# Two layers of mixers on one core: the recurrence's output projection as three one-pass products over split operands

## The reference

```
out = (yn + bonus) * g                 # 512 x 1024, from the recurrence
y   = out @ w_out                      # w_out: 1024 x 1024
x   = layernorm(ALPHA * x + (1 + gt1) * y, ln_g, ln_b)
hin = x * (1 + sc2) + sh2              # input of the feed-forward block ff0
y   = (silu(hin @ w_gate) * (hin @ w_up)) @ w_down
```

## Time and profile before

| | |
|---|---|
| time, median of three runs | 2893.52 us |
| lowest and highest run | 2893.15 and 2893.71 us |
| span of the profiled execution (first to last instruction) | 2893.6 us |
| TensorE busy | 2759.3 us, 95% |
| weight loads of TensorE | 2007.4 us, 69% |
| VectorE busy | 1360.4 us, 47% |
| ScalarE busy | 1013.0 us, 35% |
| GpSimd busy | 300.0 us, 10% |
| mean granted clock of TensorE | 0.976 |

### The profile page before, as it was taken

How to read it: one execution, slowest core, us unless ns; L and a number is a source line. 1 busy time by engine, 2 the same in 40 slices (tenths; PEclk the granted TensorE clock), 3 DMA queues, 4 the chain that set the end, 5 groups by cost and what they waited for, 6 DMA issues and landing times.

```text
span 2893.6 us, 46447 instructions
## 1 busy us (share of the span) xinstructions
PE 2759.3 (95%) x19096; PEld 2007.4 (69%) x19096; DVE 1360.4 (47%) x2285; ACT 1013.0 (35%) x1570; POOL 300.0 (10%) x250
## 2 busy tenths in 40 slices
PE   7999998899999989989999999999999899999999
PEld 3566666468888634678888778888465567788886
DVE  6566566253333257663333444433244776344335
ACT  5334333144332223644432332222011574232223
POOL 3232323010000002310000010000000131000000
PEclk9999999999999999999999999999999999999999
DMA  5334333222232111022232122232021002222331
GB/s 223 108 125 137 131 124 119 102 88 101 90 117 86 61 52 51 10 94 96 92 112 100 64 73 101 91 111 106 32 102 58 1 9 78 90 101 87 114 111 59
DMA packets 46292, 261.07 MB, mean 90 GB/s; under 512 B 5128, under 2 KB 7576, under 8 KB 26168
## 3 DMA queue, kind: packets, MB, share of 16 engines
q1 hardware_dynamic: 45128, 254.23, 25.0%
q10 hardware_dynamic: 1008, 4.57, 0.4%
HBM read 256.63 MB, written 2.15 MB: 89 GB/s over the span
## 4 chain that ended last, share of the span: by engine, by line
PE 89%; DVE 4%; ACT 3%; POOL 1%; issue 1%; DMA 1%; SPq 0%; DVEq 0%; ACTq 0%; POOLq 0%; PEld 0%; PEldq 0%
PE psum L214 87%; PE psum L2064 2%; DMA ada_first<-in_ada_first 1%; POOL branch_in L564 1%; POOL ysum L562 0%; DVE residual L1539 0%; ACT L608 0%; POOL join L557 0%; DVE residual L1531 0%; ACT yg L642 0%; DVE Y_pairs L770 0%; ACT ln_in L1494 0%; ACT nsa_probs L2100 0%; DVE ln_stat L1523 0%; DMA weights<-in_cmp_w 0%
## 5 line engine op out<-in xcount | busy, mean ns | idle before, releaser
L1657 ACT ACTIVATE ffn_weights_hi<-weights 128x1024 fp32r<-128x1024 f32 (+1 forms) x128 | 145.9, 1142 | 490.7 <-PE psum L214 490.7
L214 PE MATMUL psum<-ffn_in_hi,ffn_weights_hi 128*128 128x512 f32 x768 | 304.8, 397 | 12.4 <-DVE ffn_weights_lo L1660 7.8
L214 PE MATMUL psum<-ffn_in_hi,ffn_weights_lo 128*128 128x512 f32 x768 | 301.8, 393 | 0.0
L214 PE MATMUL psum<-ffn_in_lo,ffn_weights_hi 128*128 128x512 f32 x768 | 301.8, 393 | 0.0
L1657 ACT ACTIVATE ff_weights_hi<-weights 128x1024 fp32r<-128x1024 f32 (+1 forms) x120 | 137.7, 1147 | 433.4 <-PE psum L214 433.4
L214 PE MATMUL psum<-ff_in_hi,ff_weights_hi 128*128 128x512 f32 x704 | 277.4, 394 | 11.5 <-DVE ff_in_lo L1545 7.2
L214 PE MATMUL psum<-ff_in_lo,ff_weights_hi 128*128 128x512 f32 x704 | 276.5, 393 | 0.0
L214 PE MATMUL psum<-ff_in_hi,ff_weights_lo 128*128 128x512 f32 x704 | 276.2, 392 | 0.0
L1660 DVE TENSOR_TENSOR ff_weights_lo<-weights,ff_weights_hi 128x1024 fp32r<-128x1024 f32 (+1 forms) x116 | 156.2, 1347 | 253.5 <-ACT ff_weights_hi L1657 253.5
L1660 DVE TENSOR_TENSOR ffn_weights_lo<-weights,ffn_weights_hi 128x1024 fp32r<-128x1024 f32 (+1 forms) x126 | 166.9, 1326 | 110.5 <-ACT ffn_weights_hi L1657 110.5
L214 PEld LDWEIGHTS psum<-ffn_in_hi,ffn_weights_hi 128*128 128x128 f32 x768 | 146.2, 190 | 47.5 <-DVE ffn_weights_lo L1660 9.1
(11 more groups left out here) (519 smaller groups left out, 4878.4 us busy)
## 6 DMA issues: line engine op xcount, KB each, us to landing
weights<-in_ff_in SPq DMA_DIRECT2D x44, 1024.0 KB, 4.7
weights<-in_ffn_in SPq DMA_DIRECT2D x44, 1024.0 KB, 4.7
weights<-in_ada SPq DMA_DIRECT2D x80, 512.0 KB, 3.5
weights<-in_ff_out SPq DMA_DIRECT2D x16, 1408.0 KB, 6.0
weights<-in_ffn_out SPq DMA_DIRECT2D x16, 1408.0 KB, 6.0
weights<-in_rwkv SPq DMA_DIRECT2D x8, 1152.0 KB, 5.6
weights<-in_fox_qkv SPq DMA_DIRECT2D x4, 1536.0 KB, 6.4
weights<-in_rwkv SPq DMA_DIRECT2D x8, 640.0 KB, 4.0
```

Source lines behind the costliest of these rows:

```text
L214: return nc.tensor.matmul(out, lhsT, rhs, start=start, stop=stop)
L1657: return nc.scalar.activation(sp_.hi[u][:, 0:width], slot[s][:, u * width:(u + 1) * width], ACT.Copy)
```

## The change

`project` is removed, and `rwkv_out` goes through `split_project` with a new flag, `by_tile`. A new function, `recurrence_parts`, splits the eight tiles of the recurrence's output: the high parts on ScalarE, the low parts of the even tiles on VectorE and those of the odd ones on GpSimd. It also splits the first tile of weights, between them. With `by_tile`, TensorE waits in its first output tile for each input tile by itself, and VectorE waits for each quarter of the residual at the top of every second tile.

`residual_again` loads the residual in four transfers of 512 KB on SP's queue. Its piece is added to SP's program ahead of the piece that loads the weights. The scaling by ALPHA moves to GpSimd, in four instructions of 128x1024, behind the low parts. The steps of `gated` and `split_project` move to shared semaphores (the three `gated` lines are left out below).

```diff
--- before.py
+++ after.py
@@ -135,10 +135,10 @@
 
         in_turn = {}
 
-        def steps_again(name, names):
+        def steps_again(name, names, turns=1):
 
             s, base = in_turn.get(name) or (sem(name), 0)
-            in_turn[name] = s, base + 2 * len(names)
+            in_turn[name] = s, base + (turns + 1) * len(names)
             return Steps(s, names, base)
 
         waited = sem("waited")
@@ -1375,67 +1375,58 @@
                     nc.gpsimd.tensor_tensor(x[:, j, :], x[:, j, :], self.scaled[0], ALU.add).then_inc(*self.pool_did.step(f"add{j}"))
 
 
-        def project(name, stream, sources, ready, factor, x_ready=()):
-            n = KT // 2
-            pe_done = steps(f"{name}_pe", ["product0", "product1"])
-            sums = Sums(name, not isinstance(factor, float))
-            loads = [Loads(s, n, pe_done, f"product{s}") for s in range(2)]
+        def residual_again(ready):
+            pool_done = steps("again_pool", [f"scaled{q}" for q in range(4)])
 
             def sp(sp):
-                for s in range(2):
-                    sp.wait_ge(*loads[s].vacated())
-                with sp.Fori(0, n) as i:
-                    for s in range(2):
-                        sp.wait_ge(*loads[s].vacated(i))
-                        sp.dma_start(loads[s].slot(row(stream, i * 2 + s)), row(stream, i * 2 + s)).then_inc(*loads[s].arrival)
-
-            def pe(pe):
-                pe_done.enter(pe)
                 for r in ready:
-                    pe.wait_ge(*reached(*r))
...
-            return sums
-
-
-        def residual_again(ready):
-            act_done = steps("again_act", ["scaled"])
+                    sp.wait_ge(*reached(*r))
+                for q in range(4):
+                    sp.dma_start(x[:, 2 * q:2 * q + 2, :], d["x"][:, 2 * q:2 * q + 2, :]).then_inc(x_in[q], 16)
+
+            def pool(pool):
+                pool_done.enter(pool)
+                for q in range(4):
+                    pool.wait_ge(x_in[q], 32)
+                    nc.gpsimd.tensor_scalar(x[:, 2 * q:2 * q + 2, :], x[:, 2 * q:2 * q + 2, :], ALPHA, None, ALU.mult).then_inc(
+                        *pool_done.step(f"scaled{q}"))
+
+            phase(sp=sp)
+            return pool, [(pool_done, f"scaled{q}") for q in range(4)]
+
+        def recurrence_parts(y, parts, halves, ready):
+            act_done = steps("recurred_act", [f"hi{k}" for k in range(KT)])
+            dve_done, pool_done = steps("recurred_dve", [f"lo{k}" for k in range(0, KT, 2)]), steps("recurred_pool", [f"lo{k}" for k in range(1, KT, 2)])
 
             def act(act):
                 act_done.enter(act)
-                for r in ready:
-                    act.wait_ge(*reached(*r))
-                act.dma_start(x[:, :, :], d["x"][:, :, :]).then_inc(x_in[0], 16)
-                act.wait_ge(x_in[0], 32)
-                nc.scalar.activation(x[:, :, :], x[:, :, :], ACT.Copy, scale=ALPHA).then_inc(*act_done.step("scaled"))
-
-            phase(act=act)
-            return act_done, "scaled"
+                act.wait_ge(*reached(*ready))
+                halves.first_hi(act, 0)
+                for k in range(KT):
+                    if k == 2:
+                        halves.first_hi(act, 1)
+                    nc.scalar.activation(parts[0][:, k, :], y[:, k, :], ACT.Copy).then_inc(*act_done.step(f"hi{k}"))
+
+            def lo(eng, k, done):
+                eng.wait_ge(*act_done(f"hi{k}"))
+                own = nc.gpsimd if k % 2 else nc.vector
+                own.tensor_tensor(parts[1][:, k, :], y[:, k, :], parts[0][:, k, :].bitcast(F32), ALU.subtract).then_inc(*done.step(f"lo{k}"))
+
+            def dve(dve):
+                dve_done.enter(dve)
+                halves.first_lo(dve, 0)
+                for k in range(0, KT, 2):
+                    if k == 4:
+                        halves.first_lo(dve, 1)
+                    lo(dve, k, dve_done)
+
+            def pool(pool):
+                pool_done.enter(pool)
+                for k in range(1, KT, 2):
+                    lo(pool, k, pool_done)
+
+            phase(act=act, dve=dve, pool=pool)
+            return [[(pool_done if k % 2 else dve_done, f"lo{k}") for k in range(4 * u, 4 * u + 4)] for u in range(2)]
 
 
         def layer_norm(name, scope, layer, half_layer, sums, following, units=None):
...
-        def split_project(halves, stream, source, ready, factor, x_ready, units_free=None, into=None, gain=None, later=None, following=None, roots=None):
+        def split_project(halves, stream, source, ready, factor, x_ready, units_free=None, into=None, gain=None, later=None, following=None, roots=None, by_tile=False):
 
 
             name, split, loads = halves.name, halves.split, halves.loads
@@ -1877,7 +1868,7 @@
             n = KT // 2
             half = len(source) // 2
             width = half * P
-            pe_done = steps(f"{name}_pe", ["half0", "product0", "half1", "product1"])
+            pe_done = steps_again("projected_pe", ["half0", "product0", "half1", "product1"], n)
             sums = Sums(name, not isinstance(factor, float), into, gain, later, roots)
             PART = ("half", "product")
 
@@ -1903,14 +1894,14 @@
                         pe.wait_ge(*sums.dve(f"sum{j - 2}"))
                     for u, part in enumerate(PART):
                         pe.wait_ge(*lo_split.unit(i, s, u))
-                        if j == 0 and not roots:
+                        if j == 0 and not roots and not by_tile:
                             for r in ready[u]:
                                 pe.wait_ge(*reached(*r))
                         for k in range(half):
                             if roots:
                                 roots.between(pe, j, u, k)
-                                if j == 0:
-                                    pe.wait_ge(*reached(*ready[u][k]))
+                            if j == 0 and (roots or by_tile):
+                                pe.wait_ge(*reached(*ready[u][k]))
                             if j == KT - 1 and u == 1 and k == half - 2:
                                 sums.first_tiles(pe)
                             last = three_passes(ps[:, roots.BANKS[s][u] if roots else s, :], split, u, k, source[u * half + k],
@@ -1942,10 +1933,12 @@
                 if units_free:
                     for u in range(2):
                         halves.first_lo(dve, u)
-                for r in x_ready:
+                for r in () if by_tile else x_ready:
                     dve.wait_ge(*reached(*r))
                 for j in range(KT):
                     i, s = j // 2, j % 2
+                    if by_tile and j % 2 == 0:
+                        dve.wait_ge(*reached(*x_ready[j // 2]))
                     if j == KT - 1:
                         sums.add_square(dve, j - 1)
                         if following:
@@ -3101,8 +3094,13 @@
                 xs, lora, mix_pe, mix_act, mix_dve = time_mix_inputs(scope, hin)
                 yout, rec_done, name, turn = recurrence(scope, hin[:, :, 1:T + 1], xs, lora, mix_pe, mix_act, mix_dve)
             recurred = (rec_done, name, turn)
-            scaled = residual_again([recurred])
-            summed = project("rwkv_out", "rwkv_out", [yout[:, k, :] for k in range(KT)], [recurred], (0, GT1), [scaled])
+            with ExitStack() as scope:
+                halves = Halves("rwkv_out", Split("rwkv_out_weights", scope, KT // 2), KT, KT // 2)
+                parts = parts_of("recurred", scope)
+                scale, scaled = residual_again([recurred])
+                summed = split_project(halves, "rwkv_out", [(parts[0][:, k, :], parts[1][:, k, :]) for k in range(KT)],
+                                       recurrence_parts(yout, parts, halves, recurred), (0, GT1), scaled, by_tile=True)
+                phase(pool=scale)
         with ExitStack() as outer:
             source = parts_of("ff0_in", outer)
             units = Halves("ff0", Split("ff0_weights", outer), 2 * KT, HT // 2)
```

More of the change, by code:

```diff
@@ L1375, in add @@
                     nc.gpsimd.tensor_tensor(x[:, j, :], x[:, j, :], self.scaled[0], ALU.add).then_inc(*self.pool_did.step(f"add{j}"))
-        def project(name, stream, sources, ready, factor, x_ready=()):
-            n = KT // 2
-            pe_done = steps(f"{name}_pe", ["product0", "product1"])
-            sums = Sums(name, not isinstance(factor, float))
-            loads = [Loads(s, n, pe_done, f"product{s}") for s in range(2)]
-            def sp(sp):
-                for s in range(2):
-                    sp.wait_ge(*loads[s].vacated())
-                with sp.Fori(0, n) as i:
-                    for s in range(2):
-                        sp.wait_ge(*loads[s].vacated(i))
-                        sp.dma_start(loads[s].slot(row(stream, i * 2 + s)), row(stream, i * 2 + s)).then_inc(*loads[s].arrival)
-            def pe(pe):
-                pe_done.enter(pe)
-                for r in ready:
-                    pe.wait_ge(*reached(*r))
```

(8 more changed lines are left out.)

## The result

The changed kernel takes 2901.52 us (median of 20 runs, 2895.63 to 2908.68), the kernel before 2895.48 us (median of 20, 2891.86 to 2901.65). The ratio is 1.002, with a 95% interval of 1.0012 to 1.0028: 5.8 us slower. A second set of 12 runs gave 1.0014 (1.0003 to 1.0025), 4.1 us. The forecast was + 3.5 us and 2897.0 us, in a range up to 2900.5; the time lies 1.0 us beyond the range's end. By the mark of 0.2% that the prediction set (2899.3 us) the kernel is slower, to which it had given 0.16.

A forecast was written before the change was run, and what follows sets the result against it. TensorE was taken as the bound, busy 2759.3 of 2893.6 us. Won 11.4 us, lost 9.3 to the transfer and 6.05 to the first tile, less 0.4 in the norm: + 3.5, 2897.0 us, range 2891.0 to 2900.5.

The forecast's parts named there:

- The base: Whole kernel: the profiled span stands 0.1 us above the median of 2893.52, so a span of 2897.1 means 2897.0 us.
- The clock: Low-clock loss in the projection's second output tile and gain in the feed-forward block's second: half of each, cancelling.
- rival 4: Low clock well into the projection's second tile, 3.0 us lost; with both gains behind it failing, 2900.4 us; chance 0.11.
- The transfer: Start of the projection: first weights queue behind 2 MB of residual and land 9.3 us after 530.35; 9.3 us lost.
- Rival 2: Start of the projection: weights not held back by the residual's bytes, 4.1 us earlier, 2892.9 us; chance 0.08.
- The first tile: Projection's first output tile: the second starts 13.0 us after the first weights land; 6.05 us lost.
- Rival 1: First output tile: VectorE and GpSimd don't exclude each other, 3.7 us less, 2893.3 us, no change; chance 0.17.
- Exclusion: First output tile: VectorE's and GpSimd's subtractions from SBUF take turns, leaving 7.7 us of them in a row.
- Rival 5: First output tile: GpSimd held up at every turn, subtractions at twice 1.29 us, 5.1 us added, 2902.1 us; chance 0.05.
- The tiles: Projection's output tiles: 5.44 us each instead of 6.87, saving 11.4 us over eight.
- the norm's 0.4 us: Norm behind the projection: 11.14 us here against 10.77 behind `dsa_out`, so 0.4 us taken off.
- The sum: Whole change: projection ends 3.95 us later, less 0.4 behind it, so + 3.5 us and 2897.0 us; chance 0.54.

## Why the prediction missed, step by step

**The base, which failed.** The step was: "The profiled span stands 0.1 above the median of 2893.52, so the predicted time is 2897.0". I took the span for a time. In the 65 runs of the kernel before that stand beside the experiments the time is on average 1.8 us longer than its own span, so a span of 2893.6 belongs to a time of 2895.4, which is also the median of the 20 runs (2895.48). So the profiled execution was not one of the three runs (2893.71 us at most), for which the text on the time before takes it. And the three lie in the lower half of the 20. My effect of + 3.5 on this base is 2899.0. The range was 2 us too low with it; moved up by them it would have held the time, which the clock's term below, at its measured size, would not have done alone (2901.3). Three runs within 0.6 us had hidden that runs of this kernel spread over 10.

**The clock, which was undersized.** The term was "half of each": 0.85 us of loss in the second tile, 0.85 of gain in the feed-forward block's, cancelling. Measured: the stretch from the second tile to the last product took 40.94 us against 7 x 5.44 + 1.2 = 39.3, so the loss is 1.7 us. It came in four of four profiles with a pause of 2.40 to 2.54 us (40.8 to 40.9 us); with pauses of 0.71 and 0.99 us that stretch took 39.3, and without a pause the clock stayed full. The gain behind it did come in the first profile (clock 1.00 over 621 to 628 us, 0.76 in its twin) and did not in the second (0.76). It is a matter of the execution, also in the other kernels: four at 1.00, one at 0.89, five at 0.76 in ten profiles, both of the kernel before among the five. So half of the gain was right, and half of the loss was not: TensorE is stopped in each execution at the same place. The mechanism is rival 4's, with 1.7 us lost of its 3.0, and both of its gains failing in one of two profiles. The Trainium skill, "TensorE: Matmul & The Clock Gate", section "HAM oscillation — how this bites in real kernels", has products that starve fall back to the slow clock; the trace agrees: after the one stop of 2.40 us the granted clock was 0.50 over 558 to 561 us, from 1.5 us after the restart.

**The transfer, right.** I had 9.35 us for weights behind the residual; the two profiles have 9.81 and 9.31. Rival 2 (their bytes pass the residual's) is refuted by the pair of experiments with the order and the queue changed: 0.03 and 5.02.

**The first tile, right by two errors that cancelled, which is luck.** Counted from A, the instant at which the first weights are there, I had the second tile at A + 13.0; measured, A + 12.6. Below that total, GpSimd's low parts ended at A + 7.8 and not at A + 9.65. A GpSimd subtraction that VectorE does not hold up takes 1.16 us and not 1.29, and VectorE's pieces added 1.4 us to GpSimd's four and not 4 x 0.65, since the last of them runs behind GpSimd's last. And scaling 128x1024 takes 2.77 to 3.2 us and not 1.35, because I scaled it up from a row of another form, one with two operations. The first quarter was done at A + 11.0, exactly as predicted and for sizes that were both wrong. Rival 1 (no exclusion) had the low parts end at A + 7.15, nearer to what was measured than my own 9.65, though its mechanism did not come; its time was further off, since it took the scaling from the same row.

**Exclusion, right for the subtractions, too much for the scaling.** I took the 1.81 us row as the whole of GpSimd's instruction. The Trainium skill, "SBUF — State Buffer", section "Who interferes with whom", has the second one wait for the whole of the first, which is what I took. For two subtractions the runs agree: in each of the six profiles in which both engines subtract, a VectorE subtraction that met one of GpSimd's ended 0.55 us behind it, however early it had begun (1.77, 1.58 and 1.77 us for 0.69). For the scaling with one operation they do not: at 554.87 VectorE met a scaling that had begun at 554.82 and took 2.77 us, and lost only 0.83 us (1.52 for 0.69). If its work takes the same 0.55 us there, it was let in 1.03 us after the scaling's start; the first meeting in the kernel with all low parts on VectorE gives the same 1.03, and subtractions that began later in a scaling lost nothing. In the form with two operations, which takes 1.06 us, VectorE again waited for the whole (it ended 0.54 us behind). Rival 5, where each turn is held up to twice 1.29 us, did not come: GpSimd's four took 1.16, 1.29, 1.55 and 1.73 us.

**The tiles, right; the norm's 0.4 us, in one pair of two.** The tiles take 5.44 us each from the third on. The norm and the start of the feed-forward block took 26.75 us (597.39 to 624.14) against 27.11 before, 0.36 less in the first pair; in the second it was equal. In the ten profiles the shorter norm (10.76 us from the last update to the block's first product, against 11.07 or more) and the clock of 1.00 behind it come together, in the same four; why, no run shows.

**The sum.** The stage grew by 5.6 and 5.1 us in the two pairs where I had 3.95; from R to sparse attention 3.55 and 3.36 remained. The timed effect is 5.8 and 4.1 us, and the means of all 32 runs of the changed kernel and all 97 of the kernel before (2901.72 and 2896.81) are 4.9 us apart. Of what stands between, 0.3 us lies outside the span (2.1 us between span and time in the kernels whose low parts go to GpSimd, 1.8 in the others). So of the 4.5 us by which the forecast time was missed, 2.0 are the base, 0.8 the clock in the second tile and 0.3 this; the rest can't be told from chance with these intervals.

## What to carry to other kernels

When a stage needs one small transfer to begin and a large one only later, put the small one first, ahead of the wait of the large one as well: here that was worth 9 us of the stage, about half of it the order on the queue and half the early issue, nearly what the three-pass products save (8 x 1.43 = 11.4 by the rows). Put a wait at the instruction that needs its data, not at the top of the loop, since what stands behind it may feed the bound engine (3.8 us here). And set the sum on the base of the same kind as the time that is asked for: span to span, time to time.

## What the runs showed that I had not expected

- GpSimd multiplies 128x1024 by a constant in 2.77 us when the instruction has one operation, and in 1.35 us on average (5.42 / 4) when it has two, 1.06 us where VectorE does not hold it up. ScalarE does it in 0.97 (3.89 / 4, from its timeline).
- Two subtractions of 128x512 on VectorE and GpSimd run one after the other: VectorE's ends 0.55 us behind the end of GpSimd's in every meeting. GpSimd's one-operation scaling keeps VectorE out for the first 1.03 of its 2.77 us only, worked out from that 0.55; the two-operation form for all of its 1.06 us. So the slow form costs GpSimd's own time and hardly VectorE's.
- After a pause of TensorE of 2.4 to 2.5 us there is a stretch of about 3 us at 1.2 GHz, 1.5 us after the restart in two profiles and at once in two; after the pauses of 0.71 and 0.99 us there is none.
- The time of one kernel moves by up to 13 us from run to run (2895.63 to 2908.68 in 20 runs), where this change is worth 5. The mean granted clock moves with it: of the 35 runs of the kernel before, the shortest (2891.06 us) had 0.977 and the longest (2905.92) 0.972.
